# A decoder step with expert retrieval: a third weight slot in place of spread-out norm weights and chunk bias

## The chip, the cores and the metric

The kernel runs on one NeuronCore of a Trainium2 chip. Its metric is the time of one execution on the device in microseconds (us). All arithmetic is in float32.

## What is computed

One layer of a decoder works on 1024 prompt tokens and 32 sample tokens (8 sequences of 4 new tokens), with a model width of 1024. Cut to what matters here:

```python
proj = rmsnorm(x, norm1_g) @ w_in            # q | k | v | u, vc | memory q | 3 gates
a_swa   = sliding_window_attention(q, k, v)  # window 128, 8 heads, 2 kv heads
a_chunk = u * (tril(chunk_ws) @ rmsnorm(gelu(vc), chunk_norm_g) + chunk_bs)
a_mem   = attention(qm, memory keys, memory values)       # 256 memory tokens
h = x + sum_j(sigmoid(gate_j + b_gate_j) * (a_j @ w_branch_out[j])) @ w_out
n = rmsnorm(h, norm2_g)
q = n @ peer_wq                              # 8 heads x 2 halves of 128
e, g = top16 of the pair sums of the top16 scores of each half    # 128 experts a token
h = h + sum_e(g[e] * gelu(n . peer_u[e]) * peer_v[e])
y = rmsnorm(h, final_norm_g)
```

Each token fetches its own 128 rows of 4 KB from each of peer_u and peer_v. That is 1.1 GB of gathers, against 206 MB of everything else.

## The kernel before

The tokens are cut into nine tiles: eight of 128 prompt tokens (0 to 7) and one of the 32 sample tokens (8). The tiles form four groups: (0), (1, 2), (3, 4, 5), (6, 7, 8). The work before the experts is called the front; it runs once for each group, so all dense weights are read four times.

The experts of a tile run in 32 steps (8 for the sample tile, which is packed onto all partitions), 264 steps in all. A step gathers four rows of peer_u and four of peer_v for each of 128 tokens, 4.2 MB. GpSimd (POOL) issues the gathers (`gather_u`, `gather_v`, L1958 and L1970) into two rings, `u_ring` and `v_ring`, each two steps deep. VectorE (DVE) takes the dot products with the normed h (L1859), which lies in two PSUM banks of its own (`n2_cur`). ScalarE (ACT) makes the gelu and, for the rows that TensorE adds, diagonal matrices (L1490). TensorE (PE) adds such rows with a matmul (L1271); the other rows are added by DVE (L1873). `ON_VECTOR` says which, none to three of four in a step.

Only the front of group 0 runs with no experts beside it. The front of group g + 1 is cut into units (a block of a projection, the scores of a tile, a gate, and so on), and a planner at build time, `spread_out`, lays these units over the steps of group g. It takes costs for PE and DVE from a table (`costs`) and what must be a step apart (`waits_a_step`) or not earlier than a step (`not_ahead_of`). Steps may take 16.9 units of its time in group 0, 14.2 in group 1, 11.6 in group 2 and 10.0 in group 3. So the front of group 1 (2 tiles) falls on steps 0 to 30, that of group 2 on steps 32 to 92, and that of group 3 on steps 96 to 187. Each engine executes its part of all units in this one order.

In the plan of before, the units around the change stand so: step 0 holds queries 9 to 15 of group 0, the keys of head pair 1 of tile 0 and the turn of tile 1; steps 3 to 6 hold the blocks and values of group 1; steps 6 to 12 its attention (`scores`, `exps`, `divide`, `probs`, `mix`), steps 12 to 21 its 24 gates, steps 22 and 23 `out`. For group 2 the attention falls on steps 44 to 53, the gates on 53 to 76. For group 3 the attention of the prompt falls on steps 112 to 119, that of the sample (`smp_mem` first at step 122) on 119 to 134, the gates on 135 to 158; steps 159 to 165 hold nothing of the front, as `load_hb` of tile 6 may not stand ahead of step 166.

Every result of PE in the front goes to a PSUM bank by rotation: the n-th result (a spot, `SPOT`) takes bank `TURN[n]`. The 102 spots before step 0 rotate over six banks; from step 0 on two of the six are `n2_cur`, and the spots rotate over four. PE waits (`free`) until the bank's last user has signalled (`left`). As the order is fixed, a spot that is not emptied stops PE at the fourth spot after it.

Weights come in 94 loads (`LOADS`), issued by SyncE (SP). The first 25 (group 0) use six slots: two of `w_ring` and four in the rings, which are still empty. From load 25 on there are two slots of 2 MB, by turns, and a load is issued when the last unit that uses the load two before it has left PE. A load is 2 MB (`vc`, `u`, `q`, `mq`, `o`, `wq`), 1 MB in two DMAs (`kv`) or 1.5 MB (`d`, two gates).

The weights norm2_g, final_norm_g and the chunk bias come from memory copied to all 128 partitions (`norm2_g`, `final_g`, `chunk_b`: 4, 4 and 2 KB a partition). After `out`, `norm_h` on DVE multiplies h by norm2_g into `n2` (L1741), PE turns this (`turn_h`, L1207), ACT empties the banks into `xnT` (L1454), and the queries follow (L1218). `start_tile` (L1852) makes `n2_cur` from h, and `finish` (L1890) multiplies by final_g. `spatial` on DVE adds chunk_b (L1584) and multiplies by u (L1594).

Of the kernel before, what the change touches and what calls it, by code (L numbers as in the profile page):

```python
# [12 lines left out]
P = 128  # L13
# [60 lines left out]
WIDEST = 3 * P  # L74
# [20 lines left out]

def feed(t):

    return t if t == 0 else t + MT
# [15 lines left out]

def front_units(g):
# [10 lines left out]
    out += [("block", g, WK + 1 + n) for n in range(CG)]  # L126
# [23 lines left out]
    out += [("gate", g, i, j) for i in range(DC) for j in gate_order(i)][1 if g == 0 else 0:]  # L150
# [7 lines left out]
    out += [("query", g, n) for n in range(2 * PH)]  # L158
# [26 lines left out]
def with_first_keys(g):  # L185
# [3 lines left out]
    tail = 2 * PH - 5  # L189
# [17 lines left out]
def costs(u):  # L207

    kind = u[0]
    W = tokens(u[1]) if kind in ("block", "gate", "query") else P  # L210
# [3 lines left out]
    if kind == "gate":  # L214
        return (DC + BC) * W * column, W * 2.8e-3
    return dict(turn=(2.0, 1.4), values=(2.0, 0), chunk=(7.0, 0), spatial=(1.2, 1.4), scores=(5.2, 7.3), probs=(6.0, 1.4), mix=(5.4, 0.6),
                out=(7.0, 0.7), turn_h=(2.0, 0), keys=(2.0, 0), scale=(0, 1.8), chunk_norm=(0, 1.6), divide=(0, 4.2), norm_h=(0, 2.2),
# [5 lines left out]
def waits_a_step(u):  # L223
# [8 lines left out]
    if kind == "scores":  # L232
        return [("block", group_of(n[0]), WK)]
# [73 lines left out]
def not_ahead_of(u):  # L307
# [43 lines left out]
def build_steps():  # L351
# [21 lines left out]
    steps.append((TOTAL, []))  # L373

# [26 lines left out]
def spots(u):  # L401
# [36 lines left out]
TAKEN = [TURN[:n].count(TURN[n]) for n in range(len(SPOT))]  # L438

# [17 lines left out]
def weight_loads():  # L457

    out = []
    for g, tiles in enumerate(GROUP_TILES):  # L460
        end = tiles[-1]
        out += [(("vc", g), ("chunk", end)), (("u", g), ("block", g, WK + CG))]
        if g == 0:
            out += [(("mem", 0), ("mem_k", 1)), (("mem", 1), ("mem_v", 1))]
        out += [(("q", g), ("block", g, 3)), (("mq", g), ("block", g, 7)), (("kv", g), ("values", end))]
        out += [(("d", g, k), ("gate", g, *divmod(2 * k + (k > 0), NBR))) for k in range(DC * NBR // 2)]
        out += [(("o", g, h), ("out", end, h)) for h in range(2)]
        out += [(("wq", g, r), ("query", g, 4 * r + 3)) for r in range(4)]
# [11 lines left out]

def w_slot(n):

    return (n - WIDE) % 2 if n >= WIDE else FIRST_SLOTS[(n - WIDE + 2) % SLOTS_W]


def w_next(n):

    same = [m for m in range(n + 1, min(n + SLOTS_W + 1, len(LOADS))) if w_slot(m) == w_slot(n)]
# [58 lines left out]
def build(nc, t):  # L547

    ctx = ExitStack()
    with ctx:  # L550
# [13 lines left out]
        chunk_g, chunk_b = keep("chunk_g", CW), keep("chunk_b", CG, P)  # L564
# [3 lines left out]
        norm2_g, final_g, subT = keep("norm2_g", D), keep("final_g", D), keep("subT", 2, NK)  # L568
# [4 lines left out]
        w_ring = keep("w_ring", 2, WSLOT)  # L573
# [23 lines left out]
        sums = keep("sums", 4)  # L597
        n_dump = keep("n_dump", D, dt=BF16)
# [4 lines left out]
        eps, newton = keep("eps", 1), keep("newton", 3)  # L603
# [1487 lines left out]
```

## Time and profile before

| | us |
|---|---|
| median of 3 runs | 3373.37 |
| lowest, highest | 3368.38, 3374.26 |
| the profiled execution | 3373.66 |
| its span, first to last instruction | 3371.9 |
| PE busy in the span | 2811.1 (83%) |
| DVE busy | 2491.4 (74%) |
| POOL busy | 2123.3 (63%) |
| ACT busy | 711.7 (21%) |
| moved by DMA | 1317.05 MB, mean 391 GB/s |

Busy times are of one execution under the profiler. A matmul of f32 operands shows as two records (the expert matmuls, 1356 of them, as 2712), and a transpose as one. A busy PE is one with work in flight, not one at its peak. PEclk 1.00 is the clock level of 2.4 GHz in a whole window and 0.50 that of 1.2 GHz; values between are means over both. The DMA share is the mean busy share of the core's 16 DMA engines. It can pass 1.00 a little.

### The profile page before, as it was taken

To read this page: it belongs to the slowest core of one execution; us is meant where nothing else is said; L and a number is where in the kernel's file an instruction comes from. 1 tells how busy PE (TensorE), PEld (TensorE's weight loads), DVE (VectorE), ACT (ScalarE), POOL (GpSimd) and SP (SyncE) were. 2 spreads that over 40 slices of the span, in tenths; PEclk is the share of its full clock that TensorE was granted. 3 is DMA by queue.
4 is the path that set the end of the run, shared out by engine and by line. 5 is a ranking of instruction groups with operands and counts; after the bars stand their busy time and mean duration, and the time that the engine had idled before them with its cause. 6 is when DMAs were issued, how large, how long until landed. Compare 5 with 4: busy or idle time off the path is not lost.

```text
span 3371.9 us, 31005 instructions
## 1 busy us (share of the span) xinstructions
PE 2811.1 (83%) x9134; PEld 1579.4 (47%) x9134; DVE 2491.4 (74%) x5834; ACT 711.7 (21%) x1826; POOL 2123.3 (63%) x2128
## 2 busy tenths in 40 slices
PE   8988998899898988979877788878887777777775
PEld 6866685645454543535544555533443333333320
DVE  2277876789898888768888777767877667777764
ACT  2232211221411112222222111111221211221211
POOL 0045655556776666666677666667667777777775
PEclk9999999999999998989987799989998889989988
DMA  8779999999999999999999999999999999999998
GB/s 313 287 292 368 363 401 396 406 382 407 365 405 410 411 406 402 403 402 395 407 395 409 409 410 410 410 406 392 406 399 396 410 409 409 404 400 407 409 392 321
DMA packets 374295, 1317.05 MB, mean 391 GB/s; under 512 B 37984, under 2 KB 42848, under 8 KB 374112
## 3 DMA queue, kind: packets, MB, share of 16 engines
q0 software_dynamic: 304608, 1108.41, 83.5%
q1 hardware_dynamic: 69520, 206.66, 15.9%
q8 instruction: 75, 1.23, 0.1%
q14 instruction: 92, 0.75, 0.1%
HBM read 1303.64 MB, written 12.26 MB: 390 GB/s over the span
## 4 chain that ended last, share of the span: by engine, by line
POOL 28%; PE 22%; DMA 21%; issue 14%; DVE 13%; ACT 2%; DVEq 0%; POOLq 0%; SPq 0%; ACTq 0%
DMA v_ring_sb<-peer_v,i_all_sb 15%; POOL u_ring_sb L1958 14%; POOL v_ring_sb L1970 14%; PE ps L1271 8%; DVE u_ring_sb L1859 5%; PE ps L1182 4%; DMA u_ring_sb<-peer_u,i_all_sb 3%; DVE h_buf_sb L1873 2%; PE ps L947 2%; PE ps L1187 2%; PE ps L1218 2%; PE ps L1197 2%; PE ps L965 1%; DMA v_ring_sb<-peer_v,i_packed_sb 1%; ACT area_sb L1354 1%
## 5 line engine op out<-in xcount | busy, mean ns | idle before, releaser
L1271 PE MATMUL ps<-v_ring_sb,diag_sb 128*128 128x512 f32 x2712 | 1395.6, 667 | 422.4 <-DMA v_ring_sb<-peer_v,i_all_sb 380.2
L1958 POOL DMA_INDIRECT u_ring_sb<-peer_u,i_all_sb x1024 | 1029.8, 1006 | 740.8 <-DVE u_ring_sb L1859 286.1
L1859 DVE SCALAR_TENSOR_TENSOR u_ring_sb<-u_ring_sb,ps 128x1024 f32<-128x1024 f32 x1056 | 1252.2, 1216 | 244.5 <-DMA u_ring_sb<-peer_u,i_all_sb 211.6
L1970 POOL DMA_INDIRECT v_ring_sb<-peer_v,i_all_sb x1024 | 1026.3, 1002 | 455.7 <-issue 277.4
L1271 PEld LDWEIGHTS ps<-v_ring_sb,diag_sb 128*128 128x128 f32 x2712 | 560.3, 213 | 1166.3 <-issue 633.3
L1873 DVE SCALAR_TENSOR_TENSOR h_buf_sb<-v_ring_sb,c_sb,h_buf_sb 128x1024 f32<-128x1024 f32 x346 | 444.7, 1285 | 275.3 <-DMA v_ring_sb<-peer_v,i_all_sb 253.4
L1490 ACT ACTIVATE diag_sb<-ident_sb,c_sb 128x128 f32<-128x128 f32 x678 | 226.0, 392 | 1401.2 <-DVE c_sb L1869 1385.4
L1182 PE MATMUL ps<-xnT_sb,w_ring_sb 128*128 128x256 f32 (+3 forms) x1280 | 328.7, 410 | 1.6 <-DVE feats_sb L1657 1.6
L1182 PEld LDWEIGHTS ps<-xnT_sb,w_ring_sb 128*128 128x128 f32 x1280 | 234.1, 191 | 99.5 <-issue 28.3
L1218 PE MATMUL ps<-xnT_sb,w_ring_sb 128*128 128x256 f32 (+3 forms) x896 | 222.0, 407 | 5.2 <-DMA w_ring_sb<-w_q 4.4
L1218 PEld LDWEIGHTS ps<-xnT_sb,w_ring_sb 128*128 128x128 f32 x896 | 162.7, 194 | 67.0 <-issue 11.0
L1507 ACT ACTIVATE gelu_sb<-act_sb 128x4 f32<-128x4 f32 x264 | 54.0, 205 | 648.1 <-DVE u_ring_sb L1859 647.6
L947 PE MATMUL ps<-xnT_sb,w_ring_sb 128*128 128x256 f32 (+3 forms) x688 | 175.0, 413 | 2.5 <-DMA w_ring_sb<-w_vvc 2.5
L1187 PE MATMUL ps<-feats_sb,w_ring_sb 128*128 128x256 f32 (+3 forms) x640 | 170.1, 409 | 0.0
L947 PEld LDWEIGHTS ps<-xnT_sb,w_ring_sb 128*128 128x128 f32 x688 | 126.5, 192 | 51.4 <-issue 7.2
L1187 PEld LDWEIGHTS ps<-feats_sb,w_ring_sb 128*128 128x128 f32 x640 | 117.2, 190 | 40.5
L1197 PE MATMUL ps<-w_ring_sb,area_sb 128*128 128x512 f32 (+1 forms) x256 | 117.0, 613 | 9.1 <-DMA w_ring_sb<-w_out 6.0
L1869 DVE TENSOR_TENSOR c_sb<-gelu_sb,g_all_sb 128x4 f32<-128x4 f32 x256 | 42.8, 167 | 63.6 <-ACT gelu_sb L1507 30.2
L1859 DVE DVE_READ_ACCUMULATOR u_ring_sb<-u_ring_sb,ps 128x1 f32 x1056 | 87.0, 82 | 0.0
L1197 PEld LDWEIGHTS ps<-w_ring_sb,area_sb 128*128 128x128 f32 (+1 forms) x256 | 47.9, 189 | 77.1 <-issue 70.3
L1436 ACT ACTIVATE area_sb<-ps,gate_b_sb 128x128 f32<-128x128 f32 (+3 forms) x96 | 45.6, 476 | 169.0 <-PE ps L1182 159.9
L1721 DVE SCALAR_TENSOR_TENSOR area_sb<-area_sb,ps 128x128 f32<-128x128 f32 (+3 forms) x64 | 27.5, 430 | 61.2 <-PE ps L1187 55.3
(266 smaller groups left out, 2123.2 us busy)
## 6 DMA issues: line engine op xcount, KB each, us to landing
w_ring_sb<-w_d SPq DMA_DIRECT2D x40, 1536.0 KB, 10.5
w_ring_sb<-w_q SPq DMA_DIRECT2D x14, 2048.0 KB, 20.3
w_ring_sb<-w_b SPq DMA_DIRECT2D x10, 2048.0 KB, 14.7
u_ring_sb<-peer_u,i_all_sb POOLq DMA_INDIRECT x1024, 14.1
v_ring_sb<-peer_v,i_all_sb POOLq DMA_INDIRECT x1024, 14.2
w_ring_sb<-w_out SPq DMA_DIRECT2D x6, 2048.0 KB, 19.8
feats_sb<-x SPq DMA_DIRECT2D x12, 512.0 KB, 23.2
u_ring_sb<-w_d SPq DMA_DIRECT2D x4, 1536.0 KB, 7.1
```

The lines of the kernel that those rows point to most:

```text
L947: last = mm(bank("block", g, n)[:, 0:W], w[:, c, :], xnT[:, c, 0:W], start=c == 0, stop=c == DC - 1)
L1182: last = mm(bank("gate", g, i, j)[:, 0:W], w[:, c, :], xnT[:, c, 0:W], start=c == 0, stop=c == DC - 1)
L1187: last = mm(bank("proj", g, i, j)[:, 0:W], w[:, DC + c, :], feats[:, branch + c, 0:W], start=c == 0, stop=c == BC - 1)
L1197: last = mm(bank("out", x, half)[0:R, :], merged[:, c, W], w[:, c, :], start=c == 0, stop=c == DC - 1)
L1218: last = mm(bank("query", g, n)[:, 0:W], w[:, c, n % 4 * P:(n % 4 + 1) * P], xnT[:, c, 0:W], start=c == 0, stop=c == DC - 1)
L1271: last = mm(ps[0:M, half, :], diag[:, n % 2, j, 0:M], v_ring[:, n % 2, j, half * 512:(half + 1) * 512], start=opens, stop=closes)
L1490: A.add(fn(diag[:, (n - 1) % 2, j, 0:M], (ident if M == P else idents)[:, :], ACT.Copy, scale=c4[:, (n - 1) % 2, j:j + 1]), diags, TENSOR_ ...
L1507: A.add(fn(gelu4[:, n % 2, :], act4[:, n % 2, :], ACT.Gelu), gelus, n + 1)
L1859: V.add(v.scalar_tensor_tensor(u, u, 1.0, n2_cur[:, :], ALU.mult, ALU.mult, accum_out=act4[:, n % 2, j:j + 1]), dots, NB * n + j + 1)
L1873: V.add(v.scalar_tensor_tensor(h_buf[:, x % 2, :], v_ring[:, n % 2, j, :], c4[:, n % 2, j:j + 1], h_buf[:, x % 2, :], ALU.mult, ALU.add), ...
L1958: g.indirect_dma_start(u_ring[:, n % 2, j, :], None, t["peer_u"], index(n, j)).then_inc(u_in[n % 2][j], 16)
L1970: g.indirect_dma_start(v_ring[:, n % 2, j, :], None, t["peer_v"], index(n, j)).then_inc(v_in[n % 2][j], 16)
```

## The change

The copies of norm2_g, final_g and chunk_b on all partitions go. Their values come as rows of 128 into unused partitions of `ws_T_smp`. PE spreads them over the partitions when they are due, with matmuls whose stationary operand is a column of the identity, repeated 128 times. Two spots (`grow`) are added before each tile's first step, for norm2_g, and two before its `finish`, for final_g. The chunk bias is added by PE in `spatial`, one more matmul for each of the four channel groups. norm2_g is no longer multiplied into h before the turn: PE turns h itself, and DVE, no longer ACT, empties the banks with a multiplication by norm2_g as a column. In the sample tile `spatial` has a semaphore between its matmuls.

The memory set free holds `w_small`, a third weight slot of 1.5 MB (12 KB a partition) for `kv` and `d` loads from load 25 on. A load takes the slot among those it fits in that was last given out longest ago. That puts `kv` and four of twelve `d` loads of each of the groups 1 to 3 in it, 15 loads. The first of them, `kv` of group 1, is sent at the unit ("mix", 0), ahead of the constants, in the front of group 0.

The plan's costs change (`norm_h` 2.2 to 0.9 of DVE, `turn_h` 0 to 1.4), `turn_h` now stands ahead of `norm_h`, and ("smp_mem", 0) may not stand ahead of step 131. The queries of group 3 go to other memory. The code also learns to cut a group's matmuls into shares; here each group has one share, so the matmuls are those of before. Likewise no tile's `values` moves, since in no group a tile and the tile three after it are both found.

```diff
+SMALL = SLOTS_W
+def weight_slots():
+    out = [FIRST_SLOTS[(n - WIDE + 2) % SLOTS_W] for n in range(WIDE)]
+    last = {0: 0, 1: 1, SMALL: -1}
+    for n in range(WIDE, len(LOADS)):
+        fits = (0, 1, SMALL) if LOADS[n][0][0] in ("kv", "d") else (0, 1)
+        k = min(fits, key=lambda slot: last[slot])
+        last[k] = n
+        out.append(k)
+    return out
-    return (n - WIDE) % 2 if n >= WIDE else FIRST_SLOTS[(n - WIDE + 2) % SLOTS_W]
+    return W_SLOTS[n]
...
+    at = {n: us for n, us in steps if n is not None}
+    for x in range(TILES):
+        if x:
+            at[BATCHES * x - 1].append(("grow", "norm2", x))
+        else:
+            at[0].insert(0, ("grow", "norm2", x))
+        at[BATCHES * (x + 1) + 2 if x < PTILES else TOTAL - 2].append(("grow", "final", x))
...
+    if u == ("smp_mem", 0):
+        return [BATCHES * 4 + 3]
...
     out += [("square_h", t) for t in tiles]
+    out += [("turn_h", t) for t in tiles]
     out += [("norm_h", t) for t in tiles]
-    out += [("turn_h", t) for t in tiles]
... SP, at ("mix", 0)
+                        load_w(W_SLOTS.index(SMALL))
                         load_hb(0)
... PE, spatial
-                    last = mm(bank("spatial", x)[:, c * P:c * P + R], vc[0:R, k, c * P:(c + 1) * P], w, start=True, stop=True)
+                    last = mm(to, vc[0:R, k, c * P:(c + 1) * P], w, start=True, stop=False)
+                    if R == P:
+                        last = mm(to, ident[32:32 + CG, 32 + c:33 + c].broadcast_to([CG, P]), chunk_rows, start=False, stop=True)
... PE
+            def grow(kind, x):
+                rows, first = (norm2_rows, 96) if kind == "norm2" else (final_rows, 64)
+                for h in range(2):
+                    pe.wait_ge(*free("grow", kind, x, h))
+                    for c in range(4):
+                        at_c = first + 4 * h + c
+                        last = mm(bank("grow", kind, x, h)[:, c * P:(c + 1) * P],
+                                  ident[first:first + DC, at_c:at_c + 1].broadcast_to([DC, P]), rows, start=True, stop=True)
+                    last.then_inc(f_mm, 1)
... DVE, turn_h
+                    V.add(v.tensor_tensor(xnT[:, 4 * h:4 * h + 4, W], bank("nturn", x, h).rearrange("p (c n) -> p c n", c=4)[:, :, 0:R],
+                                          wide(norm2_col[:, 4 * h:4 * h + 4], 4, R), ALU.mult), *left("nturn", x, h))
... DVE, norm_h
-                V.add(v.tensor_tensor(n2[k][0:R, :], h_new(x), norm2_g[0:R, :], ALU.mult), n2_ready, x + 1)
... DVE, start_tile (finish likewise, with "final")
-                V.add(v.scalar_tensor_tensor(n2_cur[:, :], h_buf[:, x % 2, :], root_h[:, x:x + 1], norm2_g[:, :], ALU.mult, ALU.mult))
+                for h in range(2):
+                    part = slice(h * 512, (h + 1) * 512)
+                    dve.wait_ge(f_mm, upto("grow", "norm2", x, h))
+                    V.add(v.scalar_tensor_tensor(n2_cur[:, part], h_buf[:, x % 2, part], root_h[:, x:x + 1],
+                                                 bank("grow", "norm2", x, h), ALU.mult, ALU.mult), *left("grow", "norm2", x, h))
... DVE, spatial
-                    V.add(v.tensor_tensor(gated, bank("spatial", x).rearrange("p (c n) -> p c n", c=CG), chunk_b[:, :, :], ALU.add),
-                          *left("spatial", x))
```

## Rows read from the trace of the kernel before

**Rows 1.** The page: busy times, GB/s in 40 slices of the span, the two DMA queues.
```profile
PE 2811.1 (83%) x9134; PEld 1579.4 (47%) x9134; DVE 2491.4 (74%) x5834; ACT 711.7 (21%) x1826; POOL 2123.3 (63%) x2128
...
GB/s 313 287 292 368 363 401 396 406 382 407 365 405 410 411 406 402 403 402 395 407 395 409 409 410 410 410 406 392 406 399 396 410 409 409 404 400 407 409 392 321
...
q0 software_dynamic: 304608, 1108.41, 83.5%
q1 hardware_dynamic: 69520, 206.66, 15.9%
```

**Rows 2.** Windows: stretch, length, busy us of PE, PEld, DVE, ACT, POOL; PEclk, DMA share, GB/s.
```profile
50.00:100.00 50.00, 44.14 (x284) 35.52 (x283) 11.32 (x26) 12.35 (x42) 0.00 (x0) 0.93 0.59 222
100.00:150.00 50.00, 50.00 (x450) 50.00 (x449) 8.69 (x30) 7.33 (x21) 0.00 (x0) 1.00 0.81 286
...
350.00:400.00 50.00, 47.06 (x201) 30.81 (x200) 45.96 (x82) 16.76 (x49) 33.35 (x31) 1.00 0.91 338
...
450.00:500.00 50.00, 50.00 (x218) 40.93 (x217) 35.45 (x58) 8.47 (x19) 24.69 (x25) 1.00 1.01 402
...
700.00:750.00 50.00, 50.00 (x152) 26.69 (x151) 42.57 (x96) 21.17 (x39) 31.33 (x30) 1.00 0.97 368
...
900.00:950.00 50.00, 44.58 (x169) 25.55 (x168) 44.92 (x71) 17.18 (x52) 36.34 (x35) 0.97 0.97 366
...
1700.00:1750.00 50.00, 44.04 (x148) 23.01 (x149) 41.78 (x88) 16.89 (x50) 36.27 (x35) 0.90 1.00 385
...
2000.00:2050.00 50.00, 43.33 (x140) 26.72 (x139) 38.74 (x103) 6.07 (x18) 31.80 (x33) 0.97 1.03 410
```

**Rows 3.** Timeline from 176 us: start, us, engine, line, operation, count, idle time before and releaser.
```profile
176.84 1.23 DVE L1741 TENSOR_TENSOR area_sb<-h_buf_sb,norm_g_sb 128x1024 f32<-128x1024 f32 x1
...
178.12 1.09 PE L1207 MATMUL ps<-ident_sb,area_sb 128*128 128x128 f32 x8 [2.19 <-DVE area_sb L1741]
...
180.00 10.66 PE L1218 MATMUL ps<-xnT_sb,w_ring_sb 128*128 128x128 f32 x80 [0.79 <-issue]
```

**Rows 4.** Timeline, 190 to 225 us: group 0's last queries and step 0.
```profile
190.50 1.06 PE L1234 MATMUL ps<-subT_sb,area_sb 128*128 128x128 f32 x8
...
196.75 9.10 PE L1218 MATMUL ps<-xnT_sb,v_ring_sb 128*128 128x128 f32 x80
...
210.41 1.29 DVE L1852 SCALAR_TENSOR_TENSOR ps<-h_buf_sb,root_h_sb,norm_g_sb 128x1024 f32<-128x1024 f32 x1
...
218.19 3.71 PE L931 MATMUL ps<-ident_sb,feats_sb 128*128 128x128 f32 x16 [4.77 <-DVE feats_sb L1552]
...
219.98 0.87 DVE L1752 MAX8 sv_sb<-key_scores_sb 128x8 f32<-128x128 f32 x4
...
224.37 8.66 PE L965 MATMUL ps<-w_ring_sb,xnT_sb 128*128 128x512 f32 x16 [2.46 <-DVE xnT_sb L1562]
```

**Rows 5.** Timeline, 277 to 303 us: the load of kv of group 1.
```profile
277.48 0.55 SPq L732 DMA_DIRECT2D w_ring_sb<-w_vvc  x1
...
282.07 10.52 PE L947 MATMUL ps<-xnT_sb,w_ring_sb 128*128 128x256 f32 x48
...
295.05 5.41 PE L947 MATMUL ps<-xnT_sb,w_ring_sb 128*128 128x256 f32 x16 [2.46 <-DMA w_ring_sb<-w_vvc]
...
302.68 0.16 DVE L1869 TENSOR_TENSOR c_sb<-gelu_sb,g_all_sb 128x4 f32<-128x4 f32 x1 [12.70 <-ACT gelu_sb L1507]
```

**Rows 6.** Windows of 10 us after that load and before out of group 1.
```profile
300.00:310.00 10.00, 9.48 (x59) 7.64 (x58) 7.15 (x30) 2.40 (x9) 4.55 (x5) 1.00 0.53 200
...
520.00:530.00 10.00, 3.98 (x16) 2.42 (x14) 9.37 (x15) 1.08 (x3) 5.65 (x6) 0.89 1.03 403
```

**Rows 7.** Groups by line and shape: busy us, mean ns, idle before, releasers.
```profile
L1197 PE MATMUL ps<-w_ring_sb,area_sb 128*128 128x512 f32 x224 | 102.8, 615 | 9.1 <-DMA w_ring_sb<-w_out 6.0 <-issue 3.0
...
L965 PEld LDWEIGHTS ps<-w_ring_sb,xnT_sb 128*128 128x128 f32 x112 | 21.8, 196 | 30.1 <-issue 30.1
...
L1022 PEld LDWEIGHTS ps<-k_T_sb,feats_sb 64*128 64x128 f32 x128 | 17.8, 186 | 6.4 <-issue 4.6
```

More of the change, by code:

```diff
@@ L73 @@
 NG = len(GROUP_TILES)
-WIDEST = 3 * P
+SHARES = (((0,),), ((1, 2),), ((3, 4, 5),), ((6, 7, 8),))
+MOST = max(len(tiles) for tiles in GROUP_TILES)
 WSLOT = DC * 512
@@ L93, in tokens, with shares, columns, share_of @@
     return sum(width(t) for t in GROUP_TILES[g])
+WIDEST = SHARE_WIDEST = max(tokens(g) for g in range(NG))
+def shares(g):
+    return range(len(SHARES[g]))
+def columns(g, s):
+    first, last = SHARES[g][s][0], SHARES[g][s][-1]
+    return slice(local(first), local(last) + width(last))
+def share_of(t):
+    return next(s for s in shares(group_of(t)) if t in SHARES[group_of(t)][s])
+def last_share(g):
+    return len(SHARES[g]) - 1
 def feed(t):
@@ L112, in gate_order, with gate_units @@
     return (1, 0, 2) if i == 0 else (0, 1, 2)
+def gate_units(g):
+    return [(g, i, j, s) for i in range(DC) for j in gate_order(i) for s in shares(g)]
+GATE_TURN = {u: n for g in range(NG) for n, u in enumerate(gate_units(g))}
 def front_units(g):
@@ L125, in front_units @@
     out += [("chunk_norm", t) for t in tiles]
-    out += [("block", g, WK + 1 + n) for n in range(CG)]
+    out += [("block", g, WK + 1 + n, s) for n in range(CG) for s in shares(g)]
     out += [("spatial", t) for t in tiles]
@@ L153, in front_units @@
     out += [("square_h", t) for t in tiles]
+    out += [("turn_h", t) for t in tiles]
     out += [("norm_h", t) for t in tiles]
-    out += [("turn_h", t) for t in tiles]
     if PTILES in tiles:
         out += [("pack_root", 0)]
-    out += [("query", g, n) for n in range(2 * PH)]
+    out += [("query", g, n, s) for n in range(2 * PH) for s in shares(g)]
     return out
@@ L209, in costs @@
     kind = u[0]
-    W = tokens(u[1]) if kind in ("block", "gate", "query") else P
+    W = columns(u[1], u[-1]).stop - columns(u[1], u[-1]).start if kind in ("block", "gate", "query") else P
     column = 1.7e-3
@@ L419, in spots @@
         return [("gate", *n), ("proj", *n)]
+    if kind == "grow":
+        return [("grow", *n, h) for h in range(2)]
     if kind == "turn_h":
@@ L438 @@
 TAKEN = [TURN[:n].count(TURN[n]) for n in range(len(SPOT))]
+for _kind in ("smp_mem", "smp_mem_mix"):
+    _first, _spot = UNITS.index((_kind, 0)), SPOT[(_kind,)]
+    _ahead = sum(len(spots(u)) for u in UNITS[:_first])
+    assert TURN[_spot] not in TURN[_ahead:_spot]
 def upto(*name):
@@ L1916, in _ @@
                       smp_mem_turn=smp_mem_turn, smp_mem_soft=smp_mem_soft, smp_mem_out=smp_mem_out, gate=gate, out=out,
-                      norm_h=norm_h, first=first, second=second, best=best, found=found, experts=experts)
+                      turn_h=turn_h, norm_h=norm_h, first=first, second=second, best=best, found=found, experts=experts)
             for n, units in STEPS:
```

295 lines of the change are left out of this document (163 added, 132 removed).

## The prediction, made before the changed kernel was run

> **What bounds the kernel now.** I read the page first, from the top. PE is busiest (83%), then DVE (74%), but the GB/s line sits on a plateau of 405 to 411 in most slices, and the two queues take 83.5% and 15.9% of the 16 DMA engines [rows 1]. So over the span the transfers bind: 1317 MB at 410 would take 3212 us of 3372. The other 160 us are the prize. By slice, (410 - rate)/410 of 84.3 us each, 70 of them lie in the first three slices (mostly before any expert runs), 18 in the last, and the rest in a few places where the rate falls below the plateau.
>
> Windows of 50 us show three kinds of stretch [rows 2]. At 2000 us PE is busy for 43.3 of 50 and the DMA moves 410: bound by transfers. At 50 to 150 us it is the other way round, PE busy 44 and 50 of 50 at 222 and 286 GB/s. At 450 both are full. The low rates under the experts are at 350 to 400 (338), 700 to 750 (368), 900 to 950 (366) and 1700 to 1750 us (385), and the slices of 363, 382, 365 and 395 tell the same. The plan puts attention or a tile's start there: steps are long on DVE and PE, the gather rings are full, and both weight slots hold loads that wait for their gates. A third slot has something to add there. In a stretch at 410, a load sent earlier only takes the place of gathers, and that gives nothing by itself.
>
> **The change part by part.** The sum is made against the profiled execution, 3373.66 us (span 3371.9 plus 1.8); it lies 0.3 above the median.
>
> *a. norm2_g out of the chain of group 0.* DVE multiplies for 1.23 us, and PE's turn waits for that; the queries start at 180.00 [rows 3]. After, PE turns h at once, and DVE's 2 multiplications take the place of ACT's copies (a DVE one of that size took 0.69 us, ACT's 0.59). Gain 1.2 us (0 to 1.3). The other eight of these multiplications lie beside transfers.
>
> *b. Chunk bias on PE.* Four more matmuls of 128 columns for a tile. Four of this size, eight records, took 1.06 us [rows 4]. In tile 0 PE works without a break, so 1.1, and 0.1 for the transpose of norm2_g's rows: 1.2 lost (0 to 1.3). In tiles 1 and 2 (step 3) PE is also without a break: 2.1 lost (0 to 2.1). The tiles 3 to 8 are in stretches at 405 or more: 0; without that cover they would cost 6. DVE is spared 0.69 us a tile.
>
> *c. The first spread of norm2_g.* Eight matmuls, 2.1 us of PE, put in front of query 9. They are the first spots of the rotation over four banks, so queries 9 and 10 take the other two, and query 11 needs the bank back. DVE gives it back in `start_tile`, which runs at 210.41, behind the whole first choice of experts [rows 4]. Query 8 ends at about 198.6, the spread at 200.7, query 10 at 204.3; then PE waits until 211.1, some 6.8 us. Queued behind that are queries 11 to 15 (9.10/5 = 1.8 us each), the keys of pair 1 (1.06) and the turn of tile 1. ACT waits for query 11 before the squares of tiles 1 and 2, and GpSimd for queries 11 and 15 before its first gathers of peer_v, which by its order are due at 212.8 and 223.5 and so are hardly late. The cover is the idle 4.77 and 2.46 us that PE has there now. Query 15 ends at 220.1 if the clock holds and at 222 to 224 if it is at 1.2 GHz after the wait, as after the idle time before the chunk of tile 1 now. The keys reach DVE at 222 to 225 in place of 219.98, and the chunk starts 2 to 5 us late, but warm; I count 1.8 given back, as much as the slow clock costs in d. I take 2.8 lost (0 to 6).
>
> *d. kv of group 1 preloaded.* Now sent at 277.48, it lands at 295.05. PE waits 2.46 us and then needs 5.41 us for 16 records; 48 records took 10.52 just before, so 3.5 is normal, and the granted clock fell in between. DVE, waiting on PE through ACT, idles for 12.70 us [rows 5], and the DMA falls to 200 GB/s in the next 10 us, a deficit of 5.1 us [rows 6]. After, these weights have been there since about 90 us, loaded in a stretch at 222 GB/s. Gain 2.5 + 1.9, so 4.4 (0 to 5.1).
>
> *e. The other spreads.* Two pairs for each tile, 2.1 us each, 38 us of PE in all. Most lie at 400 GB/s and more. Two, for final_g at steps 34 and 98, fall where PE is busy throughout and the rate is low (368 at 700 us; the slice of 395 from 1517). Half of their 4.2 us: 2.1 lost (0 to 4.2). DVE's halves cost some 0.1 us more than one instruction: 0.
>
> *f. Prefetch through attention.* One more `d` load, 1.5 MB or 3.8 us at 410, can land before the gates. In group 2 the window of 366 alone has 2.2 MB to spare, but the load is sent some 50 us earlier at full rate, where DVE is nearly full too; I take 2.5 of 3.8 gained. In group 3 the deficit near 1735 is 3 us, and the load is sent into a full stretch: 1.0 gained (0 to 2.9). In group 1 there is room for more than one load at 350 to 400 (338 GB/s is 3.6 MB short), but the gates after it are bound by PE as well (50.00 of 50 at 402 GB/s [rows 2]). There the slot also frees w_out's load three gates earlier: it makes PE wait 6.0 us now [rows 7], at 524 to 530, with the DMA at 403 [rows 6]. Together 3.0 gained (0 to 9.7): a DMA at 402 of 410 lets 145 us shrink by 3. The slot's other loads gain and cost nothing: the same bytes move.
>
> *g. Fewer bytes.* 1.25 MB of copies go, 1 MB of them at 222 GB/s, where nothing waits for transfers: 0 (gain up to 0.6). The three small loads on GpSimd's queue, 0.5 us each, delay masks needed 20 us later: 0.
>
> *h. The plan.* `turn_h` and `norm_h` change places and costs by less than a step can hold. The sample's memory attention moves back nine steps, and with it the gates of group 3; but seven steps before step 166 are empty now and take this up, so `out` comes two steps later, into four empty ones before 192. At 2000 us PE has 6.7 of 50 us free at 410 GB/s. 0 (up to 4 lost, if two gates meet a tile's start).
>
> Sum: -1.2 + 1.2 + 2.1 + 2.8 - 4.4 + 2.1 - 2.5 - 1.0 - 3.0 + 0 + 0 = -3.9. Forecast 3369.8, say 3370.
>
> One might price the spreads by their 8 rows of contraction, near nothing. The trace has no matmul of so few rows; its nearest is a weight load of 64 rows, 186 ns against 196 for 128 [rows 7]. The Trainium skill ("TensorE: Matmul & The Clock Gate", LDWEIGHTS) states that a weight load takes as long for 32 rows as for 128. By that rule the sum stands; priced by rows, b, e and the spread in c would go, 7.5 us less.
>
> **The rivals.** *All prefetches pay.* For it: each low window follows a stretch in which both slots are held. Against it: where the load is sent the DMA is already at 405 to 410. Then d gives 5.1, f gives 3.8 + 2.9 + 8, and c costs 1: 3373.7 - 19.8 + 1 + 3.3 + 1 = 3359.
>
> *The banks decide (slower).* One mechanism: a pair holds two of four banks until DVE reaches `start_tile` or `finish`, and PE stands at the fourth spot behind. For it: step 0 does so for certain. Against it: later tiles have few spots between, and most starts have transfers as cover. If c costs its 6 and each of the eight other starts 2.1, that is 22.8 lost; with b and the gains of d and f as above, 3373.7 + 22.8 + 2.1 - 10.9 = 3388. With c at 6, it is past 3380.4 once a start costs 1.2 us.
>
> *Nothing moves.* The transfers bind, and only their order changes: 3371 to 3376, say 3373. For it: 2000 us and most windows. Against it: rows 5, where a load stops everything. The Trainium skill ("DMA: Bandwidth & Descriptors", Rules for kernel authors) says that two transfers serialize since both use the same 16 engines; the shares of over 1.00 in the full windows agree, and by that rule alone this rival holds.
>
> **Chances.** Forecast 0.37, all prefetches 0.29, banks 0.18, nothing 0.16. About 0.2% (6.7 us) is what a measurement tells from no change. Faster: 0.28 of the second case and 0.10 of the first, 0.38. Slower: 0.17 of the banks and 0.05 from my sizes, 0.22. Same: 0.40. The forecast's own range is 3364 to 3376. With the bounds (c +3, e +2, h +4, b 0 above; d, f and e some 14 below) and the rivals, 8 in 10 lie in 3356 to 3385.
>
> **What would show it.** PE idle for about 7 us before query 11, ended by DVE's `start_tile`, and the chunk of tile 1 at 226 to 229. No wait of PE for w_vvc near 290, and no 10 us at 200 GB/s. Spreads of 2.1 us. PE's wait for w_out gone. Rates at 300 to 400 and 870 to 930 a little higher, those at 410 unchanged. I am wrong if the time between 200 and 700 us changes by more than 8 us, if the gates of group 3 stretch the part after 1750, or if the low rates at 350 and 900 vanish.

## The result and the profile after

The changed kernel takes 3384.56 us (median of 7, 3381.14 to 3388.83), the kernel before 3372.85 (median of 7, 3368.38 to 3374.79). The ratio is 1.0035 [1.0024, 1.0047]: some 12 us slower, where 3370 was forecast. The profiled execution took 3381.14 us, its span 3379.4. The page (busy, and GB/s in 40 slices):

```profile
PE 2872.8 (85%) x9519; PEld 1631.1 (48%) x9519; DVE 2478.5 (73%) x5844; ACT 711.5 (21%) x1803; POOL 2105.5 (62%) x2130
...
GB/s 294 292 289 364 368 398 389 405 395 365 409 381 410 410 406 399 404 394 400 397 404 409 405 409 410 409 409 395 400 400 398 410 409 409 406 402 397 407 403 313
```

Against [rows 1], PE is 61.7 us busier, for 385 more matmul records. The first slices are lower (294 for 313), and the plateau is the same. So the loss is in places, not spread out. The start of group 0's turn (timeline; columns as in [rows 3]) answers to those rows:

```profile
179.59 1.07 PE L1303 MATMUL ps<-ident_sb,h_buf_sb 128*128 128x128 f32 x8 [0.90 <-issue]
180.32 1.29 DVE L1843 TENSOR_TENSOR xnT_sb<-ps,norm_col_sb 128x512 f32<-128x512 f32 x2 [0.77 <-PE ps L1303]
181.71 2.47 PE L1326 MATMUL ps<-xnT_sb,w_ring_sb 128*128 128x128 f32 x20 [1.06 <-issue]
```

PE turns h itself, and DVE multiplies on the way out, as expected. Yet the queries start at 181.71, not at 180.00. Before, they started 3.3 us after h was ready (at 176.73); here h's last half is written by the instruction at 178.79, 0.69 us long, so it is 2.2 us. But h itself is ready 2.7 us later (at 179.48). How much of that the change makes is open: with the 4-row matmuls it is ready at 178.25 in e1 below, without them at 178.00 in e9 and at 175.87 in e5. Step 0 (answers to [rows 4]):

```profile
198.85 2.05 PE L1313 MATMUL ps<-ws_T_smp_sb,ident_sb 8*128 8x128 f32 x16
...
200.83 3.84 PE L1326 MATMUL ps<-xnT_sb,v_ring_sb 128*128 128x128 f32 x32
...
210.62 1.42 DVE L1961 SCALAR_TENSOR_TENSOR ps<-h_buf_sb,root_h_sb,ps 128x512 f32<-128x512 f32 x2
...
211.53 11.16 PE L1326 MATMUL ps<-xnT_sb,v_ring_sb 128*128 128x128 f32 x80 [6.86 <-DVE ps L1961]
...
215.56 0.93 POOL L2085 DMA_INDIRECT v_ring_sb<-peer_v,i_all_sb  x1 [3.84 <-PE ps L1326]
```

This is the bank hold as forecast: a spread of 2.05 us, then PE idle for 6.86 us until `start_tile`. GpSimd's first gather of peer_v also waits, 3.84 us. The kv load of group 1 (answers to [rows 5]) and w_out (to [rows 6, 7]), from the timeline:

```profile
306.42 3.62 PE L1026 MATMUL ps<-xnT_sb,w_ring_sb 128*128 128x256 f32 x16
...
309.87 3.62 PE L1026 MATMUL ps<-xnT_sb,w_small_sb 128*128 128x256 f32 x16
...
317.09 0.37 SPq L808 DMA_DIRECT2D w_small_sb<-w_d  x1
...
528.14 0.55 SPq L808 DMA_DIRECT2D w_ring_sb<-w_out  x1
...
538.31 1.88 PE L1379 MATMUL ps<-v_ring_sb,diag_sb 128*128 128x512 f32 x4
...
540.02 5.31 PE L1292 MATMUL ps<-w_ring_sb,area_sb 128*128 128x512 f32 x12
```

The keys' 16 records on `w_small` wait for nothing and take 3.62 us in place of 5.41; `out` of group 1 follows PE's other work without a wait. Both prefetches do what they should.

What I had not forecast stands at 750 us, where the chunk mixing of tiles 3 to 5 runs. PE's timeline there:

```profile
752.67 0.38 PE L1059 MATMUL ps<-ws_T_sb,area_sb 128*128 128x128 f32 x2
752.99 0.48 PE L1061 MATMUL ps<-ws_T_smp_sb,ident_sb 4*128 4x128 f32 x2
753.40 0.49 PE L1059 MATMUL ps<-ws_T_sb,area_sb 128*128 128x128 f32 x2
753.82 0.48 PE L1061 MATMUL ps<-ws_T_smp_sb,ident_sb 4*128 4x128 f32 x2
...
755.89 1.98 PE L1379 MATMUL ps<-v_ring_sb,diag_sb 128*128 128x512 f32 x4
...
761.76 0.76 PE L1059 MATMUL ps<-ws_T_sb,area_sb 128*128 128x128 f32 x2
762.46 0.79 PE L1061 MATMUL ps<-ws_T_smp_sb,ident_sb 4*128 4x128 f32 x2
```

L1059 mixes, L1061 adds the chunk bias from 4 rows. A matmul is two records. Each matmul starts 0.42 us after the one before, where [rows 4] has 0.13 us a record, so 0.27 a matmul. A tile takes 3.22 us, where its mixing alone took 0.9 before (eight records from 751.16 to 752.05). No idle time is booked, since the ends of matmuls are modelled. From 761.76 they start 0.70 to 0.73 us apart: the granted clock has gone to 1.2 GHz, though PE shows as busy throughout from 741 to 761. Windows of 10 us (columns as in [rows 2]), first of the kernel after, then of the kernel before:

```profile
760.00:770.00 10.00, 10.00 (x28) 6.33 (x27) 9.68 (x28) 0.72 (x3) 4.40 (x5) 0.59 1.03 410
770.00:780.00 10.00, 10.00 (x25) 5.04 (x24) 4.55 (x5) 0.98 (x3) 2.25 (x3) 0.90 0.62 235
780.00:790.00 10.00, 10.00 (x32) 5.89 (x31) 6.25 (x25) 0.53 (x2) 7.37 (x8) 1.00 0.94 309
```

```profile
760.00:770.00 10.00, 10.00 (x23) 4.75 (x22) 9.58 (x30) 0.98 (x3) 7.67 (x8) 0.83 1.03 409
770.00:780.00 10.00, 10.00 (x31) 5.70 (x30) 9.64 (x27) 1.07 (x3) 5.34 (x7) 1.00 1.03 409
780.00:790.00 10.00, 10.00 (x31) 5.70 (x30) 9.04 (x14) 3.35 (x6) 7.98 (x7) 1.00 1.03 396
```

Behind the mixing stand the projections and then the weighted sums that free peer_v's ring. GpSimd's next gather shows the rest:

```profile
776.45 1.03 POOL L2085 DMA_INDIRECT v_ring_sb<-peer_v,i_all_sb  x1 [10.63 <-PE ps L1379]
```

It waited 10.63 us for PE, and so the DMA fell to 235 GB/s. By the first dot product of each step, step 40 starts 5.8 us later than before, step 42 11.0.

### The profile page after: what moved, and what is told of

The parts are those of the page before. It is cut to its first block, busy times and chain, and to the rows that moved or that the text cites. A ratio compares the mean times of both kernels' runs of the same rounds, so it can differ in the third digit from the quotient of the medians.

```text
span 3379.4 us, 31767 instructions
## 1 busy us (share of the span) xinstructions
PE 2872.8 (85%) x9519; PEld 1631.1 (48%) x9519; DVE 2478.5 (73%) x5844; ACT 711.5 (21%) x1803; POOL 2105.5 (62%) x2130
## 4 chain that ended last, share of the span: by engine, by line
PE 28%; POOL 24%; DMA 21%; issue 12%; DVE 12%; ACT 2%; SPq 0%; DVEq 0%; POOLq 0%; ACTq 0%
DMA v_ring_sb<-peer_v,i_all_sb 15%; POOL u_ring_sb L2073 12%; POOL v_ring_sb L2085 12%; PE ps L1379 9%; PE ps L1026 5%; DVE u_ring_sb L1969 5%; PE ps L1277 4%; PE ps L1326 3%; DMA u_ring_sb<-peer_u,i_all_sb 3%; PE ps L1282 2%; DVE h_buf_sb L1983 2%; DMA v_ring_sb<-peer_v,i_packed_sb 2%; PE ps L1046 1%; ACT area_sb L1462 1%; DMA feats_sb<-x 1%
## 5 line engine op out<-in xcount | busy, mean ns | idle before, releaser
L2073 POOL DMA_INDIRECT u_ring_sb<-peer_u,i_all_sb x1024 | 1012.9, 989 | 738.2 <-DVE u_ring_sb L1969 286.0
L1983 DVE SCALAR_TENSOR_TENSOR h_buf_sb<-v_ring_sb,c_sb,h_buf_sb 128x1024 f32<-128x1024 f32 x340 | 437.0, 1285 | 251.9 <-DMA v_ring_sb<-peer_v,i_all_sb 227.3
L1277 PE MATMUL ps<-xnT_sb,w_ring_sb 128*128 128x256 f32 (+3 forms) x896 | 225.5, 405 | 3.6 <-DVE feats_sb L1753 3.6
L1326 PE MATMUL ps<-xnT_sb,w_ring_sb 128*128 128x256 f32 (+3 forms) x896 | 218.9, 403 | 3.2 <-DMA w_ring_sb<-w_q 2.2
L1277 PEld LDWEIGHTS ps<-xnT_sb,w_ring_sb 128*128 128x128 f32 x896 | 161.7, 192 | 68.9 <-issue 21.1
L1326 PEld LDWEIGHTS ps<-xnT_sb,w_ring_sb 128*128 128x128 f32 x896 | 160.1, 190 | 64.5 <-issue 11.8
L1026 PE MATMUL ps<-xnT_sb,w_ring_sb 128*128 128x256 f32 (+3 forms) x640 | 163.3, 414 | 0.0
L1026 PEld LDWEIGHTS ps<-xnT_sb,w_ring_sb 128*128 128x128 f32 x640 | 117.8, 192 | 46.3 <-issue 9.7
L1282 PE MATMUL ps<-feats_sb,w_ring_sb 128*128 128x256 f32 (+3 forms) x448 | 116.2, 402 | 0.0
L1277 PE MATMUL ps<-xnT_sb,w_small_sb 128*128 128x256 f32 (+2 forms) x384 | 104.8, 426 | 0.0
L1282 PEld LDWEIGHTS ps<-feats_sb,w_ring_sb 128*128 128x128 f32 x448 | 80.8, 190 | 27.0
L1277 PEld LDWEIGHTS ps<-xnT_sb,w_small_sb 128*128 128x128 f32 x384 | 73.4, 192 | 33.1 <-issue 9.6
```

Source lines behind the costliest of these rows:

```text
L1026: last = mm(bank("block", g, n, s)[:, 0:W], w[:, c, :], xnT[:, c, C], start=c == 0, stop=c == DC - 1)
L1277: last = mm(bank("gate", g, i, j, s)[:, 0:W], w[:, c, :], xnT[:, c, C], start=c == 0, stop=c == DC - 1)
L1282: last = mm(bank("proj", g, i, j, s)[:, 0:W], w[:, DC + c, :], feats[:, branch + c, C], start=c == 0, stop=c == BC - 1)
L1326: last = mm(bank("query", g, n, s)[:, 0:W], w[:, c, n % 4 * P:(n % 4 + 1) * P], xnT[:, c, C], start=c == 0, stop=c == DC - 1)
L1983: V.add(v.scalar_tensor_tensor(h_buf[:, x % 2, :], v_ring[:, n % 2, j, :], c4[:, n % 2, j:j + 1], h_buf[:, x % 2, :], ALU.mult, ALU.add), ...
L2073: g.indirect_dma_start(u_ring[:, n % 2, j, :], None, t["peer_u"], index(n, j)).then_inc(u_in[n % 2][j], 16)
```

## The experiments

Times are medians; ratios are to the kernel before on the same chip. Differences in us are of medians and partly of different chips, on which the kernel before took 3371.0 to 3372.9, so one or two us of a difference mean nothing. Theories to begin with: the plan of steps, which had changed more than I had foreseen (P); the banks (B); the slot.

**1. The plan.** The new order of `turn_h` and `norm_h` and what `turn_h` waits for let the planner accept other rooms. Group 1 runs a step later, group 2's attention and gates three, group 3's gates nine. e1_oldplan is the kernel after with the plan of before; e2_newplan the kernel before with the plan of after.

```diff
 e1, in front_units:
+    out += [("norm_h", t) for t in tiles]
     out += [("turn_h", t) for t in tiles]
-    out += [("norm_h", t) for t in tiles]
 and costs, waits and the bound of smp_mem as before
```

> The changed kernel with the plan of the kernel before: costs, order and distances of norm_h and turn_h, and no bound on smp_mem, so that every unit but the spreads stands in the step it had. Theory P (the plan costs the time: the swap of norm_h and turn_h let the planner take 16.2 and 14.0 in place of 16.9 and 14.2, which moved the front of group 1 one step back and the gates of group 2 three): 8 to 12 us faster than the changed kernel, near the kernel before or a little under it. Theory B (the banks and the added matmuls cost it): within 4 us of the changed kernel, 8 to 14 above the kernel before.

> The kernel before with the plan of the changed kernel (only turn_h stays behind norm_h, as it must there): no spreads, no third slot. Theory P: 8 to 12 us slower than the kernel before. Theory B: within 3 us of the kernel before.

Measured: e1 3395.67, ratio 1.0072 [1.0059, 1.0086]; e2 3392.14, 1.0062 [1.0049, 1.0076]. The plan of before makes the changed kernel 11 us slower, so P falls as the cause; B had expected no more than 4 us either way, so it does not explain e1 either. e2 alone went P's way, and twice as far as P had it. Each kernel is fastest with its own plan. Where e1 loses is seen in two windows and a wait (engine, line, releaser: us, times, longest):

```profile
270.00:280.00 10.00, 10.00 (x29) 7.54 (x29) 2.97 (x5) 0.00 (x0) 0.94 (x1) 0.56 0.98 391
280.00:290.00 10.00, 10.00 (x47) 8.15 (x47) 5.67 (x7) 2.33 (x6) 3.64 (x4) 1.00 0.26 71
```

```profile
POOL v_ring_sb L2083 <- PE ps L1377: 14.4, 1, 14.4
```

Here it is the mixing of tiles 1 and 2: clock down with PE busy, then the gathers of peer_v wait for PE, then 71 GB/s.

**2. The slot and the hold.**

```diff
 e3_two_slots
-        fits = (0, 1, SMALL) if LOADS[n][0][0] in ("kv", "d") else (0, 1)
+        fits = (0, 1)
-                        load_w(W_SLOTS.index(SMALL))
 e4_hold
-            at[0].insert(0, ("grow", "norm2", x))
+            at[0].insert(at[0].index(("query", 0, 13, 0)), ("grow", "norm2", x))
```

> The changed kernel with its third slot unused: all loads from the 25th on by turns in two slots. If the third slot gives what step d and f of the prediction say, this is 7 to 11 us slower than the changed kernel; if transfers bind and only their order changes, within 3 us of it. Nothing of theories P and B changes here.

> The changed kernel with the first spread put in front of query 13 instead of query 9, so that no query waits for start_tile. Theory B: PE's wait of 6.9 us before query 11 goes, and 4 to 8 us are gained on the changed kernel. Theory P: the wait goes but less than 3 us are gained, as the plan leaves step 0 and 1 with room.

Measured: e3 3390.76, 1.0055 [1.0042, 1.0069], so the slot gives 6.2 us, between what my d and f had it (7 to 11) and nothing. e4 3378.94, 1.0019 [1.0010, 1.0028], so the hold costs 5.6. Against the kernel after, 1.0035 [1.0024, 1.0047], both intervals overlap at their ends; e12 below shows the slot's gain clear of noise. B holds for step 0, but e4 is still slower than before.

**3. The form of the bias matmuls.** In all kernels with the 4-row matmuls the clock falls near 760 us behind a PE that shows as busy; in those without, it does not (the 0.83 of the kernel before at 760 comes behind 2.18 us in which PE waited). The rows of `ws_T_smp`'s tile hold the chunk bias in partitions 32 to 35; with the tile zeroed first, a column of the identity picks row 32 + c out of all 128 just as well. GpSimd zeroes it at the start of the kernel; that line is left out below.

```diff
 e5_tall_bias (e4 and:)
-  mm(to, ident[32:32 + CG, 32 + c:33 + c].broadcast_to([CG, P]), chunk_rows, start=False, stop=True)
+  mm(to, ident[:, 32 + c:33 + c].broadcast_to([P, P]), rows_at[:, :], start=False, stop=True)
 e6_no_bias (e4 and:) that matmul left out
 e7_oldplan_hold: e1 with e4's edit
 e8_short_spreads (e4 and:) in grow
-                    for c in range(4):
+                    for c in range(1):
```

e6 adds no chunk bias, and e8's spreads fill only a quarter of their columns, so these two do not compute the layer; they are there for their times.

> The kernel after, with the first spread before query 13 (as e4_hold) and the chunk bias of the full tiles added by matmuls of 128 rows of contraction in place of 4: same number of matmuls, same columns, same result. Why: in every kernel that carries the 4-row matmuls the granted clock falls to 1.2 GHz at 758 to 773 us, in the spatial mixing of tiles 3 to 5, with TensorE busy without a break before it, and the DMA then moves 235 to 345 GB/s for 30 us; in the kernels without them it does not fall there. Theory N (the narrow matmuls let the clock fall): no half clock near 765, no hole behind it, and 3 to 8 us less than e4_hold's 3378.9, so 3371 to 3376. Theory W (only the time of the added matmuls counts): the fall and the hole stay, or go without the time changing; within 2 us of 3379. Theory L (the loss at steps 36 to 42 comes from the later plan of group 2 alone): within 2 us of 3379 too, with the hole there at full clock.

> As e4_hold, with the chunk bias of the full tiles left out: 32 matmuls of 128 columns fewer, no bias is added there (the sample's tile keeps its own). Theory N: the clock stays up at 765 and the hole behind it goes, 3 to 8 us less than 3378.9, and no more than 1 to 3 below e5_tall_bias. Theory W: 1 to 3 us below both e4_hold and e5_tall_bias. Theory L: 3378 to 3380, the hole stays.

> The kernel after with the plan of before (as e1_oldplan, 3395.7) and with the first spread before query 13 (as e4_hold). If the old plan lost because it puts the turn of tile 3 and ACT's squares behind the bank hold of step 0 (theory H: e1 was 11.5 us behind by step 8), it is then 8 to 12 us faster, 3384 to 3388, and the clock does not fall near 269. If the old plan and the third slot do not fit together (theory F), or the spatial mixing of tiles 1 and 2 drops the clock by itself in step 3 (theory N), it gains no more than the 5.6 us that the new plan gained: 3390, with the fall of the clock at 265 to 275 and the hole in the DMA behind it still there. If the plan of before were simply better by the 21 us that e2_newplan lost, it would come to 3358.

> As e4_hold, with one matmul in place of four in each spread (norm2_g and final_g then reach only a quarter of their columns; banks, waits and VectorE's halves are as before). The work of the spreads on TensorE falls from 2.05 to about 0.5 us for a pair. As I priced them, at half of the pairs in two places and nothing elsewhere, it gains 1 to 3 us: 3376 to 3378. If the spreads' work does not count at all: within 1 us of 3379. If every spread is paid in full, 17 pairs of 1.5 us: 25 us less, 3354. If the narrow matmuls of the spreads also drop the clock, the half-clock time (546 us in e4_hold) falls by some 30 us and the gain is 5 us or more.

Measured: e5 3366.12, 0.9979 [0.9970, 0.9988], 12.8 us under e4 and faster than the kernel before; more than I had expected. e6 3361.19, 0.9970 [0.9958, 0.9982], 4.9 us under e5 where 1 to 3 were expected, though the intervals overlap. e7 3397.26, 1.0071 [1.0057, 1.0084]: mending the hold gives the old plan nothing. e8 3378.58, 1.0022 [1.0013, 1.0031]: the spreads' work counts for nothing. The timeline of e5, same tile, and its windows:

```profile
741.71 0.38 PE L1060 MATMUL ps<-ws_T_sb,area_sb 128*128 128x128 f32 x2
...
741.83 0.30 PEld L1062 LDWEIGHTS ps<-ws_T_smp_sb,ident_sb 128*128 128x128 f32 x2
...
741.93 0.39 PE L1062 MATMUL ps<-ws_T_smp_sb,ident_sb 128*128 128x128 f32 x2
742.16 0.39 PE L1060 MATMUL ps<-ws_T_sb,area_sb 128*128 128x128 f32 x2
...
743.50 1.88 PE L1380 MATMUL ps<-v_ring_sb,diag_sb 128*128 128x512 f32 x4
```

```profile
760.00:770.00 10.00, 10.00 (x32) 5.85 (x31) 9.64 (x27) 0.87 (x2) 7.67 (x8) 1.00 1.03 410
770.00:780.00 10.00, 10.00 (x32) 5.71 (x31) 9.33 (x17) 2.61 (x6) 6.99 (x8) 1.00 1.02 407
780.00:790.00 10.00, 10.00 (x37) 6.00 (x36) 8.17 (x11) 3.53 (x6) 6.08 (x6) 1.00 1.02 413
```

The same eight matmuls take 1.79 us in place of 3.22, the clock stays up, and the hole in the DMA is gone. The weight loads show where the time goes. Here a load starts 0.10 us before its matmul, beside the one that runs. In the kernel after, at a change of height, it starts only with it (timeline, tile 2):

```profile
276.63 0.29 PEld L1061 LDWEIGHTS ps<-ws_T_smp_sb,ident_sb 4*128 4x128 f32 x2
276.63 0.48 PE L1061 MATMUL ps<-ws_T_smp_sb,ident_sb 4*128 4x128 f32 x2
```

**4. What else depends on it.**

```diff
 e9_after_tall: the kernel after with e5's matmul; the hold stays
 e10_tall_all (e5 and:) in grow
-  ident[first:first + DC, at_c:at_c + 1].broadcast_to([DC, P]), rows
+  ident[:, at_c:at_c + 1].broadcast_to([P, P]), rows_at[:, :]
 e11_tall_oldplan: e7 with e5's matmul
 e12_tall_two: e5 with e3's edit
```

> The kernel after, as it is, but for the chunk bias of the full tiles on matmuls of 128 rows in place of 4 (the first spread stays before query 9). Theory N (the narrow bias matmuls let the clock fall, and that alone turned the change into a loss): the 12.8 us between e4_hold (3378.9) and e5_tall_bias (3366.1) come here too, so 3384.6 - 12.8 = 3372 (3369 to 3375), no half clock at 762, and the bank hold of step 0 is still there. If mending the hold was needed for that gain: 3376 or more. If the hold costs nothing once the clock stays up: 3366.

> As e5_tall_bias, and the spreads of norm2_g and final_g by 128 rows of contraction in place of 8 as well: same count, same result. If the spreads too let the clock fall: less half-clock time than e5_tall_bias's 520 us and 2 to 5 us less time, 3361 to 3364. If they do not (e8_short_spreads, with a quarter of them, moved nothing): 3365 to 3367. If narrow matmuls are also cheaper by themselves: slower than e5, by up to 17 pairs of 1 us.

> As e7_oldplan_hold (plan of before, first spread before query 13, 3397.3), with the chunk bias on 128 rows. There the clock fell at 267 and 762 us with TensorE busy, 10 and 17 us long. Theory N alone (the old plan lost by the clock): it gains 20 us or more and comes to 3366 or below, the old plan being the better one on the kernel before by 21 us. N and F (old plan and third slot do not fit together besides): it gains 8 to 18 us, 3379 to 3389, no fall at 267 or 762. F alone: 3394 to 3399.

> As e5_tall_bias, with the third slot left unused (two slots take turns, as before). The slot was worth 6.2 us between after and e3_two_slots; if that is its worth: 3372. My prediction's d and f came to 10.9: 3377 by them. If the slot's gain was only a cure for waits that the slow clock made: 3366 to 3368.

Measured: e9 3367.59, 0.9984 [0.9975, 0.9993], 17.0 us under the kernel after by this one edit, and 4 more than e5's gain carried over (3372 expected): what was put down to the hold is mostly gone too. The two profiled executions are 11.5 us apart by their last step; of these, 5 have come by step 38, 9 come between steps 38 and 42, and the kernel after makes up some 3 later. e10 3365.98, 0.9983 [0.9974, 0.9992]: as e5, the spreads' height does not matter. e11 3369.53, 0.9994 [0.9985, 1.0003]: 27.7 us under e7, so the old plan was not unfit for the slot; it had only met the slow matmuls where nothing covers them. I had put theory N alone at 3366 and both at 3379, so it is nearly N alone. e12 3371.53, 1.0000 [0.9991, 1.0010]: the slot is worth 5.4 us here too.

**5. Rows or changes of height.** e13_grouped keeps the 4-row matmuls but issues a tile's four in a row; e14_rows32 alternates with 32 rows; e15 adds the alternation, with weights of zero, to the kernel before.

```diff
 e13_grouped (e4 and:)
+                if R == P:
+                    for c in range(CG):
+                        ...
+                        mm(to, ident[32:32 + CG, 32 + c:33 + c].broadcast_to([CG, P]), chunk_rows, start=c == 0, stop=False)
                 for c in range(CG):
-                    last = mm(to, vc[...], w, start=True, stop=False)
-                    ... the bias matmul
+                    last = mm(to, vc[...], w, start=R != P, stop=R == P and c == CG - 1)
 e14_rows32 (e4 and:)  ident[32:64, 32 + c:33 + c], rows_at[32:64]
 e15_narrow_in_before
-  last = mm(bank("spatial", x)[...], vc[...], w, start=True, stop=True)
+  last = mm(to, vc[...], w, start=True, stop=R != P)
+  if R == P:
+      last = mm(to, ident[32:32 + CG, 0:1].broadcast_to([CG, P]), chunk_b[32:32 + CG, c, :], start=False, stop=True)
```

> As e4_hold (3378.9), but in each full tile the four bias matmuls of 4 rows come first, one after another, and the four of the spatial mixing behind them: same matmuls, same result, 2 changes of height in place of 8. Theory S (TensorE can't overlap neighbours of different height, and the clock falls because of the gaps): the eight matmuls take about 2.2 us in place of 3.2, no fall of the clock near 762, 3366 to 3371. Theory R (few rows of contraction lower the clock by themselves): the clock falls as before, 3376 to 3380.

> As e4_hold, with 32 rows of contraction (28 of them zero) in place of 4 in the bias matmuls, alternating with those of 128. Theory S: any height other than 128 costs the same, a matmul and its partner still 0.83 us a pair of records, 3377 to 3381. If it is the number of rows: between 3366 and 3379, near e5_tall_bias when 32 rows are enough.

> The kernel before, with a matmul of 4 rows added behind each one of the spatial mixing of the full tiles; its weights are zero, so it adds nothing to the result, and VectorE still adds the bias. Nothing else of the change is in it: plan, slots and banks are those of before. Theory S: in the plan of before the 128 rows gave 27.7 us (e7 to e11), so it comes to 3388 to 3400, with falls of the clock near 270 and 760. If the narrow matmuls only harm together with the third slot or the spreads: 3371 to 3378.

Measured: e13 3365.42, 0.9981 [0.9972, 0.9990]; e14 3376.95, 1.0015 [1.0005, 1.0024]; e15 3394.41, 1.0068 [1.0054, 1.0082]. All three are as theory S has it. Tile 3 in e13, then in e14 (timelines):

```profile
743.03 1.15 PE L1059 MATMUL ps<-ws_T_smp_sb,ident_sb 4*128 4x128 f32 x8
744.11 1.16 PE L1063 MATMUL ps<-ws_T_sb,area_sb 128*128 128x128 f32 x8
745.11 1.88 PE L1381 MATMUL ps<-v_ring_sb,diag_sb 128*128 128x512 f32 x4
```

```profile
746.92 0.38 PE L1060 MATMUL ps<-ws_T_sb,area_sb 128*128 128x128 f32 x2
747.23 0.48 PE L1062 MATMUL ps<-ws_T_smp_sb,ident_sb 32*128 32x128 f32 x2
747.65 0.49 PE L1060 MATMUL ps<-ws_T_sb,area_sb 128*128 128x128 f32 x2
...
756.54 0.79 PE L1062 MATMUL ps<-ws_T_smp_sb,ident_sb 32*128 32x128 f32 x2
```

e13: 2.08 us with 2 changes of height; after: 3.22 with 8; e5: 1.79 with none. A change costs (3.22 - 2.08)/6 = 0.19 us. It comes in two halves: in e14 the first 32-row matmul starts 0.31 us behind its neighbour, where e5 has 0.22, and the next one 0.42 behind that. (The 2.08 us start at the first 4-row matmul, behind the first half of the first change, so 2.08 - 1.79 is one and a half changes, 0.19 each again.) 32 rows behave as 4 do, the slow clock from 756 included. And a kernel with nothing of the change but this alternation is 22 us slower; by e5 and e6 some 5 of these would be the added matmuls' own. The Trainium skill ("TensorE: Matmul & The Clock Gate", Why this matters for your kernels) says that a matmul of 32 rows takes as long as one of 128. The starts agree for 4 rows: e13's eight 4-row records start 0.11 us apart, as its eight of 128 rows do. That sentence is on a single matmul; for neighbours of two heights e14 has 0.42 us in place of 0.22.

e5, e10 and e13 are the best complete versions found, all faster than the kernel before by 0.2%, and not to be told apart.

## Why the prediction was wrong

The step that failed is b. I priced the bias matmuls by a row of four neighbours of one height (1.06 us), gave tiles 0 to 2 3.3 us in all and tiles 3 to 8 nothing, 6 at most. Four of 4 rows between four of 128 add 2.3 us to the tile, not 1.06, and the clock falls behind one to three tiles of them. That was no rival and no bound of mine; the range ended at 3385 only for the banks. The edit e9 removes 17.0 us of it. The case that I had called hidden is where it hurt: at 750 us the DMA was full, but the cover ended once GpSimd's gather stood behind PE, for 10.63 us. Of the signs that I had named, the rates of 410, which were to stay, show it (235 at 770 us); the time between 200 and 700 us, which was to tell me that I am wrong, does not (3.2 us more from step 0 to step 34). The choice to price 4 rows like 128 was right (weight loads of 183 ns at the median against 189, L1061 and L1059 after); what was left out is the neighbour of another height. The trace of before had it, at other forms (last section), and I had not compared starts.

The other terms, with what the runs gave:

- *a*, -1.2: from h to the queries 3.3 us became 2.2, so -1.0.
- *b* without changes of height, +3.3: 4.9 (e6 to e5; the intervals overlap).
- *c*, +2.8: the wait was 6.86 us for the 6.8 forecast; its price is 5.6 (after to e4) with the slow matmuls and 1.5 without (e9 to e5); in both pairs the intervals overlap.
- *d* and *f* together, -10.9: -6.2 (e3 to after) and -5.4 (e12 to e5). Mechanism right, size twice too large. PE's waits for kv and w_out went, but w_out's gates now end at 538, so only part of it reached the end.
- *e*, +2.1: three quarters of the spreads' work gave 0.4 us, which is nothing measurable.
- *h*, 0: wrong in what it says. I read the swap of `turn_h` and `norm_h` as too small to matter; the planner searches for the least room that fits, and a changed order moved whole groups of work. The new plan gains 3.4 us where the matmuls are of one height (e11 to e5, intervals overlapping) and 18.3 where they are not (e7 to e4). A plan sets what a fault meets.

So "the banks decide" gave the right sign and nearly the right time (3388) by the wrong mechanism: the later starts did not hold PE. This is who waited for the two readers of the spreads in the kernel after, `start_tile` (L1961) first and `finish` (L2003) second (us in all, times):

```profile
  PE ps L1326: 6.9, 1
```

```profile
  PE ps L1227: 9.6, 1
  PE ps L1342: 0.9, 1
```

The 9.6 us are in the sample's memory scores, and end at 1888 us. From 1870 to 1890 us the DMA moves 409 to 410 GB/s, so the transfers cover them. (That the kernel is 9.7 us behind the one before at step 120 and 4.5 ahead at step 132 is no gain: the plan has put these scores later, and by step 180 it is 5.9 behind.) No run takes this wait out. With the one edit the kernel is 4.3 us faster than before (3371.86 to 3367.59), close to the -3.9 of my sum; that is partly luck, since d and f were 5 too good and b 1.6, while c, e and h erred the other way by 1.3, some 2 and 3.4.

Open: how the 17 us divide between the changes of height themselves (8 tiles, 1.4 us each, under cover in some) and the slow clock behind them; and why the clock falls behind the alternation, of which the runs show only that it does. Open too is why e2_newplan is 21 us slower than before. It loses at the turns of the groups (step 24 is 0.7 us ahead of before, step 30 13.3 behind; step 84 1.9 behind, step 90 15.8), where DVE's multiplication by norm2_g still stands before PE's turn and now comes later in the plan. No run separated that.

## What to carry to other kernels

Price an added matmul by the neighbours that it will have, not by itself: between matmuls of another contraction height it costs the change, twice. Look for the distance between starts in the trace that you have: this change of form stood there. Put those of one height together, or pad them to the height of the rest; both took back the whole loss here. And when a planner or search sets the order, run it on the changed input before calling an edit to its tables small.

## What the hardware showed that was not expected

- Neighbouring matmuls of 128 and of 4 or 32 rows start 0.42 us apart (two records each, 128 columns, full clock), those of one height 0.22; the cost of one change is 0.19 us. All the low ones began at partition 32; none was tried at another.
- Height is not the only change that costs. In the kernel before, at full clock, four records of 512 columns take 1.72 us to the start of a neighbour of their form, and 1.81 to one whose stationary operand has 64 columns (timelines):

```profile
749.44 1.88 PE L1271 MATMUL ps<-v_ring_sb,diag_sb 128*128 128x512 f32 x4
751.16 1.05 PE L976 MATMUL ps<-ws_T_sb,area_sb 128*128 128x128 f32 x8
...
355.71 1.88 PE L1271 MATMUL ps<-v_ring_sb,diag_sb 128*128 128x512 f32 x4
357.52 1.94 PE L1056 MATMUL ps<-area_sb,v_nat_sb 128*64 128x512 f32 x8
```

- The same 0.09 us stands in that trace before a neighbour of 64 rows (340.26 to 340.79 us for one record, where two of one form start 0.43 apart), and at all 20 places where a record of the weighted sum stands right before one of 64 rows or of 64 or 32 stationary columns. There these changes are few; the chunk mixing had made eight in a tile.
- The granted clock went to 1.2 GHz behind one to three tiles of such alternation (761.76 us after, 756 in e14, 268 in e1) though the trace shows PE as busy without a break. With the same 4-row matmuls in one row (e13), it did not fall there. "PE busy" in the windows does not show these gaps; the distance between starts does.
- A stretch at 410 GB/s covers PE only as far as its rings reach: 10.63 us of PE's lateness became 235 GB/s for 10 us.
